# Warming transposes, an earlier vector turn and two weight splits on GpSimd at the head of a hybrid encoder block

## The reference

```
h = rms_norm(x, norm1_g)
[q | k | v | p] = h @ w_in                       # 512 + 128 + 128 + 512 columns
a = sliding-window attention of q, k, v, with sinks
m = trailing means of p over 2, 4, 8, 16 tokens, one linear map per group
x = x + concat([a, m]) @ w_out
x = x + (silu(gate) * val) @ w_down,   gate, val = causal_conv3(rms_norm(x, norm2_g) @ w_up)
```

## Time and profile before

| what | us |
|---|---|
| median of 3 runs (lowest to highest) | 1776.51 (1775.22 to 1776.84) |
| profiled execution, first to last instruction | 1774.4 |
| PE busy in it | 1755.5 |
| DVE, ACT, POOL busy in it | 1334.7, 805.7, 247.3 |

### The profile page before, as it was taken

The page is one execution under the profiler, slowest core; times in us unless marked ns, Lnnn a source line. Parts: engine busy times, 40 slices in busy tenths (PEclk is TensorE's granted clock), DMA queues, the critical chain, the costliest instruction groups (busy, mean ns, idle before and its releaser), DMA issues.

```text
span 1774.4 us, 23434 instructions
## 1 busy us (share of the span) xinstructions
PE 1755.5 (99%) x8490; PEld 1462.7 (82%) x8490; DVE 1334.7 (75%) x1796; ACT 805.7 (45%) x1437; POOL 247.3 (14%) x270
## 2 busy tenths in 40 slices
PE   7999999999999999999999999999999999999999
PEld 6888888888878888888888888888888888888887
DVE  5645644635779999999998998998998778865774
ACT  4554544534765444444454444444444433333321
POOL 1213212202110000000000000000004033310210
PEclk9999999999999999999999999999999999999999
DMA  8553383484445523323376223223227999976884
GB/s 324 225 220 107 114 311 110 166 290 160 164 171 186 194 84 128 133 83 95 119 251 211 72 83 96 71 84 95 72 83 235 343 343 332 314 254 211 302 286 130
DMA packets 211555, 321.73 MB, mean 181 GB/s; under 512 B 13737, under 2 KB 106097, under 8 KB 211441
## 3 DMA queue, kind: packets, MB, share of 16 engines
q1 hardware_dynamic: 192014, 267.75, 45.3%
q10 hardware_dynamic: 19427, 52.49, 7.6%
HBM read 249.93 MB, written 70.25 MB: 180 GB/s over the span
## 4 chain that ended last, share of the span: by engine, by line
PE 92%; DVE 3%; DMA 2%; ACT 2%; issue 1%; POOL 0%; ACTq 0%; DVEq 0%; POOLq 0%
PE ps L810 29%; PE ps L811 29%; PE ps L812 29%; PE ps L969 1%; PE ps L993 1%; PE ps L980 1%; PE ps L1033 1%; DMA raw<-in_w_out_dram 1%; DMA raw<-in_w_in_dram 1%; DMA gT_d<-cb 0%; DVE hT_lo L1564 0%; DVE va_lo L1788 0%; DVE w_lo L1517 0%; POOL ss_q L2043 0%; PE ps L956 0%
## 5 line engine op out<-in xcount | busy, mean ns | idle before, releaser
L810 PE MATMUL ps<-va_hi,wv 128*128 128x512 f32 x1232 | 479.8, 389 | 1.4 <-DVE va_lo L1751 0.6
L811 PE MATMUL ps<-va_lo,wv 128*128 128x512 f32 x1232 | 479.3, 389 | 0.0
L812 PE MATMUL ps<-va_hi,wv 128*128 128x512 f32 x1232 | 479.3, 389 | 0.0
L810 PEld LDWEIGHTS ps<-va_hi,wv 128*128 128x128 f32 x1232 | 231.3, 188 | 51.3 <-issue 2.8
L812 PEld LDWEIGHTS ps<-va_hi,wv 128*128 128x128 f32 x1232 | 231.3, 188 | 48.0
L811 PEld LDWEIGHTS ps<-va_lo,wv 128*128 128x128 f32 x1232 | 231.3, 188 | 47.6
L810 PE MATMUL ps<-dt_hi,ds_hi 128*128 128x512 f32 x616 | 239.6, 389 | 0.0
L812 PE MATMUL ps<-dt_hi,ds_lo 128*128 128x512 f32 x616 | 239.6, 389 | 0.0
L811 PE MATMUL ps<-dt_lo,ds_hi 128*128 128x512 f32 x616 | 239.6, 389 | 0.0
L1838 DVE SCALAR_TENSOR_TENSOR cb<-ub,cst,cb 128x1024 f32<-128x1024 f32 x176 | 219.8, 1291 | 10.1 <-ACT cb L1357 10.1
L1357 ACT ACTIVATE cb<-ub,cst 128x1024 f32<-128x1024 f32 x88 | 108.9, 1243 | 142.7 <-DVE ub L1893 86.3
(11 more groups left out here) (170 smaller groups left out, 2819.7 us busy)
## 6 DMA issues: line engine op xcount, KB each, us to landing
dg<-gT_d SPq DMA_DIRECT2D x264, 256.0 KB, 5.5
rw<-in_w_up_dram SPq DMA_DIRECT2D x84, 512.0 KB, 5.0
dw<-in_w_down_dram SPq DMA_DIRECT2D x132, 256.0 KB, 5.5
gT_d<-cb ACTq DMA_DIRECT2D x44, 512.0 KB, 2.6
raw<-in_w_out_dram SPq DMA_DIRECT2D x32, 512.0 KB, 4.1
w_hi<-wA_d SPq DMA_DIRECT2D x30, 512.0 KB, 3.3
w_lo<-wA_d SPq DMA_DIRECT2D x30, 512.0 KB, 5.2
n<-in_x_dram SPq DMA_DIRECT2D x16, 512.0 KB, 8.2
```

The lines of the kernel that those rows point to most:

```text
L810: pe.matmul(out_ap, l_hi, r_hi, start=first, stop=False, skip_group_check=True)
L811: pe.matmul(out_ap, l_hi, r_lo, start=False, stop=False, skip_group_check=True)
L812: return pe.matmul(out_ap, l_lo, r_hi, start=False, stop=last, skip_group_check=True)
```

## The change

- PE: when the first three signals of `const_pool` are there (the identity is built), it turns the identity 28 times into the last quarter of bank 0, before it waits for all nine and begins t1.
- PE: the vectors are turned ahead of tile 2 instead of tile 3 (its index t; the change's title counts it as the third).
- DVE: the copy to `cst` comes ahead of the scaling of tile 3; the low halves of units 0 and 1 are gone from it.
- POOL: makes the low half of unit 0 behind the four roots, and that of unit 1 in t1, with a semaphore of their own, `first_lo`.
- Whoever waited for the split of unit 0 or 1 (SP's raw loads and stores, PE) now waits for `first_lo`, and for later units for a `split_lo` that counts two fewer (`split_there`).

```diff
+WARM = 28
+POOL_SPLITS = 2
+        def split_there(engine, m):
+
+            if m >= POOL_SPLITS:
+                engine.wait_ge(S["split_lo"], m - POOL_SPLITS + 1)
+            elif m >= 0:
+                engine.wait_ge(S["first_lo"], m + 1)
+
@@ sync, load
-                    wait(sp, "split_lo", m - RAW + 1)
+                    split_there(sp, m - RAW)
...
-                    sp.wait_ge(S["split_lo"], m + 1)
+                    split_there(sp, m)
@@ tensor, halves_there and t1
-                    pe.wait_ge(S["split_lo"], SPLIT_NO[n] + 1)
+                    split_there(pe, SPLIT_NO[n])
...
-                        if t == 3:
+                        if t == 2:
                             vectors()
@@ tensor, before the walk
+            pe.wait_ge(const_pool, 3)
+            for i in range(WARM):
+                pe.transpose(ps[:, 0, 3 * P:], ident[:], ident[:])
             pe.wait_ge(const_pool, CONST_POOL)
@@ vector
             def n1_(a):
                 for t in range(NT):
+                    if t == 3:
+                        dve.wait_ge(const_turned, 1)
+                        v.tensor_copy(cst[:], ps[:, 0, 0:200]).then_inc(vectors_read, 1)
                     scale(0, a, t, n1)
-                dve.wait_ge(const_turned, 1)
-                v.tensor_copy(cst[:], ps[:, 0, 0:200]).then_inc(vectors_read, 1)
-                split(0)
...
-                    if a == 0 and i == 3:
-                        split(1)
@@ gpsimd
+            def n1_(a):
+                norm(0, a)
+                split(0)
+
+            def split(m):
+
+                pool.wait_ge(S["split_hi"], m + 1)
+                g_.tensor_tensor(w_lo[:, m, :], raw[:, m, :], as_f32(w_hi[:, m, :]), ALU.subtract
+                                 ).then_inc(S["first_lo"], 1)
+
+            def t1(a, h):
+                if a == 0:
+                    split(1)
```

More of the change, by code:

```diff
@@ L433, in bass_hybrid_block @@
         S = {name: sem(name) for name in (
-            "split_hi split_lo unit_used sq1 step1 rstd1 xs1 turned1 hT_hi hT_lo p_carried p_copied win_step "
+            "split_hi split_lo first_lo unit_used sq1 step1 rstd1 xs1 turned1 hT_hi hT_lo p_carried p_copied win_step "
             "mix_ready pool_done m_copied mT_step mT_ready kv_done k_squared k_summed k_step k_rstd k_scaled v_kept "
@@ L1273, in t2 @@
                     if a == NB - 1 and dt == 0:
-                        act.wait_ge(S["split_lo"], N_SPLIT)
+                        split_there(act, N_SPLIT - 1)
                         act.wait_ge(S["sq2"], NT * NB)
@@ L2100, in _ @@
             pool.wait_ge(const_pool, CONST_POOL)
-            walk(dict(n1=n1sq, n1sq=n1sq, n2sq=n2sq, pin=pin, q=q, kve=kve, inv=inv, inv1=inv1, av=av))
+            walk(dict(n1=n1_, t1=t1, n1sq=n1sq, n2sq=n2sq, pin=pin, q=q, kve=kve, inv=inv, inv1=inv1, av=av))
             def keep_halo(un):
```

## The result

| what | before | after |
|---|---|---|
| median of 21 runs (lowest to highest), us | 1775.75 (1774.78 to 1777.56) | 1778.52 (1776.32 to 1782.38) |
| ratio after to before, 95% interval | | 1.0015 [1.0009, 1.0021] |
| span of the profiled execution, us | 1774.4 | 1775.8 |
| runs whose mean granted clock of TensorE is listed below 1.000 | 0 of 21 | 13 of 21 |

The changed kernel is 2.8 us slower. That is inside the predicted range and inside the 0.2% called no difference, but it lies clear of zero, and the forecast was a gain of 0.4 us. The last line of the table is the first clue. The 8 runs with a mean clock of 1.000 have a median of 1777.4, and the 13 with 0.999 or 0.998 one of 1779.2: some lose 1.8 us more than others to something that the clock sees. The profiled execution (1777.64) is one of the first kind, so its trace shows only part of the loss.

What follows compares the result with a forecast made beforehand. PE, busy 1755.5 of 1774.4 us, bounds the kernel; 1.5 us won at the head is cut to 0.4 by unit 5's load at 39.06. 1774.4 - 0.4 = 1774.0, plus 2.1 gives 1776.1 us, range 1774.1 to 1778.6.

Steps and rivals of the forecast that it cites:

- the central claim: At kv 0's tile 2, PE waits for unit 5's raw data: 0.4 us gained of the 1.5 at the head.
- POOL I charge 0.65 for the scaling (0 to 0.65): At unit 0's split near 11.35 us, POOL loses 0.65 us to DVE's scaling of tile 3; low half done at 14.6.
- the slower rival: At pin 1's wait for unit 1's low half, POOL's subtraction is long: up to 6.5 us late, 1783.0; chance 0.04.
- The step: Ahead of kv 0's tile 2, PE is through at 37.2, waits for unit 5's raw data, goes on at 38.65.
- The clock does not stay up: Rival at pin 0: lower clock at 14.7, 0.6 us of delay at 39, 1777.1; 0.15 together with later loads.
- late loads: Rival case at unit 5's raw load: loads later by up to 1 us; chance 0.15 together with the clock.
- where the DMA engines had room: From 18 to 22 us, 328 GB/s against 409: 0.32 MB or 0.8 us lost, half taken as recoverable.
- The bound of 0.8 later: Worst case for unit 5's landing: hole unfilled, both delays and packet disorder added; other bound 1.5 us earlier.
- Behind 39 us every stage hangs on PE or on loads with several us to spare: Past kv 0's tile 2, the 0.4 us gain, or any loss, reaches the end of the kernel.
- its own sum: Whole kernel: first four cases lie between 1775.0 and 1777.5; run spread adds about 0.8 us on either side.
- The long POOL subtraction: At pin 1's wait for unit 1's low half: slower than before when it exceeds 5.9 us; chance 0.03 or 0.04.
- The 2.1 us added to the span: Whole kernel: the median stands 2.1 us above the profiled execution, making 1774.0 into 1776.1.

Runs made afterwards that it cites:

- e10_pool_first: Changed kernel with DVE's copy to `cst` waiting for unit 0's high half, so POOL always goes first; 1778.66 us, ratio 1.0015.
- e6_x_later_after: Changed kernel with block 1's tiles issued behind unit 5's raw load instead of ahead of it; 1778.91 us, ratio 1.0009.
- e11_ordered_x_later: Changed kernel with POOL's first subtraction waiting for DVE's scaling of tile 3, and block 1's tiles issued behind unit 5's raw load; 1775.45 us, ratio 0.9997.
- e13_ordered_filled: e9_ordered plus 12 identity turns on PE ahead of its wait for kv 0's tile 2; 1778.05 us, ratio 1.0012.
- e9_ordered: Changed kernel with POOL's first subtraction waiting until DVE has scaled all four tiles; 1779.10 us, ratio 1.0016.
- e1_before: The kernel before, unchanged, timed against itself as a control; 1775.81 us, ratio 1.0001.
- e4_after: The changed kernel again, unaltered, timed against the kernel before; 1778.66 us, ratio 1.0017.
- e7: Changed kernel with 12 identity turns on PE ahead of its wait for kv 0's tile 2; 1778.33 us, ratio 1.0018.
- e12_hold_unit4: e9_ordered with SP holding unit 4's raw load until DVE has made its constants; 1779.31 us, ratio 1.0021.

## Why the prediction was right and wrong

**Right, in the profiled execution, in which DVE is first.** The turns end at 7.03 (7.2 said), tile turns are about 0.118 apart, `cst` is copied at 10.52, `hT_hi` begins at 12.56 (12.4), `hT_lo` 4 to 7 run from 16.54 to 19.27 (16.3 to 19.0), POOL's subtractions take 2.91 and 2.40 (3.25 with the scaling, and 2.6), unit 0's low half is done at 14.29 (14.6), pin 1 starts at 20.21 (20.2). `hT_lo` was not disturbed by POOL. So was the central claim: the gain is cut at 39.06, where PE waits for unit 5's raw data. On the turns themselves, against the Trainium skill's "TensorE: Matmul & The Clock Gate", Part 4, 28 of them in 5.42 us cannot have run at 0.214 apart (6.0 us) throughout, and what follows them is at about 0.118; the trace decides. (The 28 took from 4.61 to 6.02 us over the profiles; seven turns of a tile took 0.95 to 0.99 behind them in all.)

**Wrong: "POOL begins at 11.35, but DVE is then scaling tile 3 until 12.0", and so "POOL I charge 0.65 for the scaling (0 to 0.65)".** The collision was seen and priced for one order alone, taken from starts 0.1 us apart in a trace of a kernel that did not have the operation. The other order costs not 0.65 us of POOL, hidden, but 2.1 us on PE's path and a low clock behind it. e10_pool_first (11 of 11 runs low) and e6_x_later_after against e11_ordered_x_later (6 to 0) show it. This should have been the slower rival: its price could be worked out from the earlier trace rows, one subtraction of 2 to 3 us ahead of the scaling.

**Wrong: PE's pause at 39 us costs only what it lasts.** The step said that PE would be through at 37.2 and wait, which it does, and then counted the wait as a loss of the gain and no more. A pause of 0.15 us became one of 1.5 to 2.8 us, and in the profiles with 2.06, 2.79 and 3.43 us of it the clock falls to 0.50 behind it, for 1.49, 1.48 and 2.65 us; in those with 1.50 and 1.46 it does not. "The clock does not stay up" was among the rivals, at 0.15 together with late loads, and was looked for at pin 0, where 1.10 us of idling spoke against it. The right rival stood at the wrong gap. e13_ordered_filled, against e9_ordered, shows that the idling is what does it. Nor was the late load harmless with the clock up: e13_ordered_filled still loses 1.4 us (1778.05 against 1776.62).

**Mis-sized: where the DMA engines had room.** I looked for it in 18 to 22 us and found 0.32 MB; the room is in 14 to 18 us, where 44 and 251 GB/s leave more than 1 MB, and it belongs to the splits of units 0 and 1, which GpSimd does not do sooner. Block 1's tiles were to leave 1.4 us earlier, at 22.2, and left at 23.43, as the issue of unit 2's high half ahead of them took 1.50 us instead of 0.76. In before they leave at 23.59, in e1_before at 23.43 too. ACT starts on unit 5 at 37.13, 37.24, 37.62, 38.11 and 38.30 in the five profiles with two splits on POOL, DVE first and the loads in their order, against 37.23 and 36.82 in before and e1_before: not 0.4 earlier but some 0.7 later. The bound of 0.8 later holds for the mean, not for the last two.

**Wrong: "Behind 39 us every stage hangs on PE or on loads with several us to spare, so the gain or loss is carried to the end."** In the profile of after PE waits 1.1 us at 503 us for a load that it did not wait for before, and POOL's work, 0.14 us early at 455 us, is 0.91 us late at 512.

**The sum, as far as it goes.** In the 8 runs of after with clock 1.000 the loss is 1.7 us; the profile of one gives -0.16 at 39 us, 1.1 of waiting at 503, and half a us more in small pieces behind 512 us. In the 13 low ones 1.8 more are lost, about what one fall of the clock cost in e4_after and e9_ordered (1.5) and a little more.

**Luck in the range.** That 1778.52 lies inside 1774.1 to 1778.6 is luck. None of its rivals gives this loss at this gap, and the upper end is not what its own sum gives: 1777.5 + 0.8 is 1778.3. (The long POOL subtraction has a chance of 0.03 in one list and 0.04 in the other.) The 2.1 us added to the span were 0.3 too many as well: in every run of the result the time stands 1.8 us above its own span, and the rest came from setting one execution against a median of three.

**Still open.** The wait of 0.5 to 1.1 us at 503 to 506 us stands in the profiles of after, e4, e7, e9 and e13 and in none of the others. All five have both splits on POOL, DVE first and block 1's tiles in the old place; but so has e12_hold_unit4, without the wait. Why a load issued at the same point, 440 us later, then takes 11.5 instead of 10.4 us is not settled, and neither are the low runs of e13_ordered_filled. Why unit 5's raw data comes later behind POOL's splits is argued from the loads' issues and not shown by a run of its own. That POOL is first in some executions of after itself is inferred from e6_x_later_after, whose head has the same program; no profile of after caught one. So how the 13 low runs of after divide between the race and the pause is not known.

## What to carry to other kernels

Before work goes to GpSimd, list what VectorE does in SBUF at the same moment, and price both orders; if the starts lie within a tenth of a microsecond, force the order with a wait or take another instruction. When an engine that was just in time becomes early, its new pause is not free for TensorE: a gain of 1.5 us that ends in front of a late load can come back as a loss of 3 (e9_ordered). Move the load first (here block 1's tiles behind it), then the work ahead of it. Here that took the loss away; a gain that could be told from zero it did not bring.

## What the runs showed of the hardware

- A VectorE scaling of 128 x 1024 (0.75 us) and a GpSimd subtraction of 128 x 1024 (2.34 us alone) do not overlap: the one that comes second lasts 2.58 to 2.93 us, whichever it is, in six profiles with starts up to 0.31 us apart.
- TensorE's granted clock fell from 1.00 to 0.50 with pauses of 2.06, 2.64, 2.69, 2.79 and 3.43 us and stayed there for some 3 to 7 us. With 1.46, 1.50 and 1.83 us it did not. Twelve transposes of the identity in the pause kept it up in the one profile taken of that.
- Where the three raw loads ahead were issued within 0.3 us of each other (14.2 to 14.5, 18.3 to 18.4, 20.8 to 21.1 us) and unit 5's own at 26.9 to 27.7, its raw data was there for ACT anywhere from 37.1 to 38.3 us, and not in the order of the issues (27.04: 38.30, 27.66: 37.24).
